# Time-mix recurrence of a two-block token model: the per-head 32x32 operands of two products laid on the diagonal of 128x128 operands by ScalarE

## What is computed

```python
def step(state, inp):
    r_t, d_t, k_t, v_t, kk_t, a_t = inp
    sa = jnp.einsum('bhij,bhj->bhi', state, -kk_t)
    state = (state * d_t[:, :, None, :] + sa[..., None] * (kk_t * a_t)[:, :, None, :]
             + v_t[..., None] * k_t[:, :, None, :])
    return state, jnp.einsum('bhij,bhj->bhi', state, r_t)
```

## Time and profile before

| | us |
|---|---|
| median of three runs (1913.79 to 1920.4) | 1918.26 |
| span of the profiled execution | 1915.1 |
| TensorE matmul busy | 1747.5 (91%) |
| VectorE busy | 1109.7 (58%) |
| ScalarE busy | 656.9 (34%) |
| recurrence stage, from the first L3680 to the end of the last L3694 | 1633.8 to 1670.4 |

### The profile page before, as it was taken

The page is one execution under the profiler, slowest core; times in us unless marked ns, Lnnn a source line. Parts: engine busy times, 40 slices in busy tenths (PEclk is TensorE's granted clock), DMA queues, the critical chain, the costliest instruction groups (busy, mean ns, idle before and its releaser), DMA issues. The chain is left out here.

```text
span 1915.1 us, 30043 instructions
## 1 busy us (share of the span) xinstructions
PE 1747.5 (91%) x12670; PEld 1304.1 (68%) x12670; DVE 1109.7 (58%) x2005; ACT 656.9 (34%) x1042; POOL 0.2 (0%) x4
## 2 busy tenths in 40 slices
PE   6898789988987899999988999999998989799998
PEld 5343256773432588888877788878887877568887
DVE  4342254452332677774478686678667465568765
ACT  3111112331111554452235544464443402145443
POOL 0000000000000000000000000000000000000000
PEclk9799899988997999999988999999999989679999
DMA  9999972289999855524310455545542312035540
GB/s 391 419 420 420 420 308 82 94 329 387 419 421 420 350 177 198 179 97 178 115 67 34 169 191 182 195 158 186 186 174 92 143 43 91 4 154 201 186 163 23
DMA packets 58189, 405.26 MB, mean 212 GB/s; under 512 B 6416, under 2 KB 7824, under 8 KB 10432
## 3 DMA queue, kind: packets, MB, share of 16 engines
q1 hardware_dynamic: 58048, 403.25, 54.4%
HBM read 402.18 MB, written 1.05 MB: 211 GB/s over the span
## 5 line engine op out<-in xcount | busy, mean ns | idle before, releaser
L2110 PE MATMUL ps<-ffn_x,ffn_wh 128*128 128x512 f32 x1408 | 348.3, 400 | 7.8 <-DVE ffn_x L2247 7.4
L2110 PEld LDWEIGHTS ps<-ffn_x,ffn_wh 128*128 128x128 f32 x1408 | 267.3, 193 | 68.3 <-DVE ffn_x L2247 7.7
L2254 DVE TENSOR_TENSOR ffn_wl<-w,ffn_wh 128x2048 fp32r<-128x2048 f32 x132 | 301.5, 2287 | 2.5 <-ACT ffn_wh L2198 1.1
L2198 ACT CAST ffn_wh<-w 128x2048 fp32r<-128x2048 f32 (+1 forms) x140 | 252.9, 1807 | 4.5 <-PEq L726 3.5
L2113 PEld LDWEIGHTS ps<-ffn_x,ffn_wl 128*128 128x128 f32 x1408 | 180.5, 191 | 6.8
L2113 PE MATMUL ps<-ffn_x,ffn_wl 128*128 128x256 f32 x1408 | 183.4, 283 | 0.0
L2213 ACT COPY ffn_part_low<-ps 128x512 f32<-128x512 f32 x88 | 51.5, 586 | 327.7 <-PE ps L2113 327.4
L2258 DVE TENSOR_TENSOR ffn_z<-ps,ffn_part_low 128x512 f32<-128x512 f32 x88 | 60.8, 691 | 149.7 <-ACT ffn_part_low L2213 149.5
L2157 PE MATMUL ps<-ffn_wh,ffn_hidh 128*128 128x512 f32 x352 | 137.7, 391 | 0.6 <-issue 0.6
L2158 PE MATMUL ps<-ffn_wl,ffn_hidh 128*128 128x512 f32 x352 | 137.4, 390 | 0.0
L2159 PE MATMUL ps<-ffn_wh,ffn_hidl 128*128 128x512 f32 x352 | 137.0, 389 | 0.0
(11 more groups left out here) (605 smaller groups left out, 2760.3 us busy)
## 6 DMA issues: line engine op xcount, KB each, us to landing
w<-in_ffn_gu SPq DMA_DIRECT2D x88, 1024.0 KB, 4.8
w<-in_moe_gu SPq DMA_DIRECT2D x60, 1024.0 KB, 22.7
w_extra<-in_moe_gu SPq DMA_DIRECT2D x48, 1024.0 KB, 26.1
w<-in_ffn_dn SPq DMA_DIRECT2D x44, 1024.0 KB, 4.8
w<-in_moe_dn SPq DMA_DIRECT2D x28, 1024.0 KB, 26.3
w_extra<-in_moe_dn SPq DMA_DIRECT2D x21, 1024.0 KB, 27.4
xn<-in_moe_gu SPq DMA_DIRECT2D x10, 1024.0 KB, 26.4
w_extra_late<-in_moe_dn SPq DMA_DIRECT2D x9, 1024.0 KB, 22.8
```

Source lines behind the costliest of these rows:

```text
L2110: return nc.tensor.matmul(pair_of(b)[:, a], high[:, s, tile(a, k)], X[:, k], start=k == 0, stop=False)
L2198: nc.scalar.copy(high[:, n % parts, at], S.buf(units[n])[:, at]).then_inc(*w_high.one())
L2254: nc.vector.tensor_tensor(low[:, s], S.buf(units[n]), high[:, s], ALU.subtract).then_inc(*w_split.one())
```

## The change

ScalarE lays the blocks of four heads on the diagonal of a 128x128 operand: for each quad q it copies all 128 partitions of the block column, scaled by a mask that is 1 on quad q and 0 elsewhere (`K.con(C_QUAD + q, 1)`), to column group q. Off the diagonal stand zeros. For the inverse this goes into a new tile `rw_tm`; for the scores it is done in place in `sc`, over the kinds 0, 2 and 3 that are used up, with kind 1 last after a wait for the other three. There are three calls of `quads_apart`, each of four ScalarE instructions: the inverse of all 32 slots (1024 elements a partition each), the scores of slots 0 to 15 and of slots 16 to 31 (512 elements each). The first two stand in `rwkv_inverse`, the third in the first chunk of `rwkv_chunks`; TensorE waits for the third ahead of chunk 4. L3680 and L3694 become four products each, of a 128x128 stationary operand with 64 columns, in place of sixteen. The last hunk of the diff makes the scratch space for dynamic DMAs smaller, which leaves room for the new tile.

```diff
--- before.py
+++ after.py
@@ -3214,15 +3214,15 @@
             rwkv_factors(K, NormAfterPost(K, post, gain, K.xn[:, :, 1:SEQ + 1]), r, k, sg, a, kk, ar, cl, low, mix_v, by_feat(kp))
             bp = sbi("rw_bp", [P, N_RC, QW])
             sc = sbi("rw_sc", [P, 32, 4, RC])
+            tm_quads = sbi("rw_tm", [P, 32, 4, RC])
             tm = flat(kk)[:, RC * RC:2 * RC * RC]
...
             rows = S.take("ln_rows")
-            rwkv_inverse(K, a, k, r, kk, ar, bp, kp, sc, bon, mix_v, v, g, wv, rows, kv, tm, nv, flat(sg), flat(K.xn))
-            tm = tm.rearrange("p (t u) -> p u t", t=RC)
-            rwkv_chunks(K, ar, cl, bp, kv, sc, tm, nv, y, flat(a), flat(sg))
+            rwkv_inverse(K, a, k, r, kk, ar, bp, kp, sc, tm_quads, bon, mix_v, v, g, wv, rows, kv, tm, nv, flat(sg), flat(K.xn))
+            rwkv_chunks(K, ar, cl, bp, kv, sc, tm_quads, nv, y, flat(a), flat(sg))
             K.retire("rs_made", "sa_ready_a", "kv_made", "kv_taken")
         return rwkv_output(K, y, low, g, rows, flat(K.xn)[:, 0:2 * D], "c_w_o", post_gain)
 
@@ -3458,7 +3458,15 @@
             receptance(7)
 
 
-def rwkv_inverse(K, bt, kt, rk, kend, ar, bp, kp, sc, bon, mix_v, v, g, wv, rows, kv, turned, nv, room, room2):
+def quads_apart(act, K, dst, src, slots):
+
+    for q in (0, 2, 3):
+        last = K.nc.scalar.activation(dst[:, slots, q], src[:, slots], ACT.Copy, scale=K.con(C_QUAD + q, 1))
+    link(act, K.act_step, last)
+    return K.nc.scalar.activation(dst[:, slots, 1], src[:, slots], ACT.Copy, scale=K.con(C_QUAD + 1, 1))
+
+
+def rwkv_inverse(K, bt, kt, rk, kend, ar, bp, kp, sc, tm_quads, bon, mix_v, v, g, wv, rows, kv, turned, nv, room, room2):
 
     nc, S = K.nc, K.stream
     bend = K.sq[:, :, 0:SEQ]
@@ -3597,9 +3605,11 @@
             take_by_values(0)
             take_by_values(1)
             act.wait_ge(*inverted.at(1))
+            quads_apart(act, K, tm_quads, turned.rearrange("p (t u) -> p u t", t=RC), slice(0, 32))
             take_by_values(2)
             take_v(range(4, N_RC))
             take_by_values(3)
+            quads_apart(act, K, sc, sc[:, :, 1], slice(0, 16))
             take_to_state(range(4))
             for n in range(4, 8):
                 take_by_values(n)
@@ -3638,7 +3648,7 @@
             vv.tensor_tensor(g[:], g[:], ln[:, 1:2].to_broadcast([P, N_RC, QW]), ALU.add)
 
 
-def rwkv_chunks(K, ar, cl, bp, kv, sc, tm, nv, y, room, room2):
+def rwkv_chunks(K, ar, cl, bp, kv, sc, tm_quads, nv, y, room, room2):
 
 
     nc = K.nc
@@ -3648,6 +3658,8 @@
         as_made, w_ready, sa_made, sa_ready = K.sig("s_made"), K.sig("s_ready"), K.sig("e_made"), K.sig("p_ready")
         sa_ready_a, rs_made = K.sig("sa_ready_a"), K.sig("rs_made")
         st_made, st_ready, y_made = K.sig("t_made"), K.sig("t_taken"), K.sig("pv_made")
+        y_quads = K.sig("tile_made")
+        whole = lambda of, slot: of[:, slot].rearrange("p q t -> p (q t)")
         quad = lambda q: slice(q * RC, (q + 1) * RC)
         place = [(a, par, q) for a in range(2) for par in range(2) for q in range(4)]
         of_par = K.ps[:, 0:2, :].rearrange("p r (j a i) -> p a r j i", j=4, i=HD)
@@ -3675,9 +3687,8 @@
                 for a in range(2):
                     for par in range(2):
                         g = 2 * a + par
-                        for q in range(4):
-                            w = W[quad(q), g * HD:(g + 1) * HD] if c else nv[0][quad(q), 0, g * HD:(g + 1) * HD]
-                            mm = nc.tensor.matmul(K.ps[quad(q), 2 + a, par * HD:(par + 1) * HD], tm[quad(q), 4 * c + g], w, start=True, stop=True)
+                        w = (W if c else nv[0][:, 0])[:, g * HD:(g + 1) * HD]
+                        mm = nc.tensor.matmul(K.ps[:, 2 + a, par * HD:(par + 1) * HD], whole(tm_quads, 4 * c + g), w, start=True, stop=True)
                     mm.then_inc(*sa_made.one())
                 if c:
                     read_state(c, 1).then_inc(*rs_made.one())
@@ -3689,9 +3700,11 @@
                         mm = nc.tensor.matmul(K.ps[64 * par:64 * par + 64, 4 + q, a * HD:(a + 1) * HD], bp[quad(q), c, g * HD:(g + 1) * HD],
                                               SA[quad(q), g * HD:(g + 1) * HD], start=True, stop=True)
                     mm.then_inc(*st_made.one())
-                for a, par, q in place:
-                    g = 2 * a + par
-                    mm = nc.tensor.matmul(K.ps[quad(q), 2 + a, P + par * HD:P + (par + 1) * HD], sc[quad(q), 4 * c + g, 1], SA[quad(q), g * HD:(g + 1) * HD],
+                if c == 4:
+                    pe.wait_ge(*y_quads.at(1))
+                for g in range(4):
+                    a, par = divmod(g, 2)
+                    mm = nc.tensor.matmul(K.ps[:, 2 + a, P + par * HD:P + (par + 1) * HD], whole(sc, 4 * c + g), SA[:, g * HD:(g + 1) * HD],
                                           start=True, stop=True)
                 mm.then_inc(*y_made.one())
 
@@ -3700,6 +3713,8 @@
             for c in range(N_RC):
                 act.wait_ge(*sa_made.at(2 * c + 2))
                 nc.scalar.copy(SA[:, P:2 * P], K.ps[:, 3, 0:P]).then_inc(*sa_ready_a.one())
+                if c == 0:
+                    quads_apart(act, K, sc, sc[:, :, 1], slice(16, 32)).then_inc(*y_quads.one())
 
         @block.vector
         def _(dve):
@@ -3977,7 +3992,7 @@
     import concourse.bacc as bacc
     from concourse.bass_utils import run_bass_kernel_spmd
 
-    nc = bacc.Bacc("TRN2", target_bir_lowering=False, num_devices=1)
+    nc = bacc.Bacc("TRN2", target_bir_lowering=False, num_devices=1, dynamic_dma_scratch_size=256)
     arrays = {f"in_{n}": a for n, a in layout({n: np.asarray(inputs[n]) for n in INS}).items()}
     ins = {n[3:]: nc.dram_tensor(n, a.shape, F32, kind="ExternalInput").ap() for n, a in arrays.items()}
     out = nc.dram_tensor("out", (P, KT, SEQ), F32, kind="ExternalOutput").ap()
```

## The result

The changed kernel takes 1926.35 us in the median of four runs (1924.18 to 1928.79), the kernel before, measured beside it, 1917.42 (1913.79 to 1920.4): a ratio of 1.0053 (95% interval 1.0040 to 1.0066), slower by 8.9 us. In a later comparison the same kernel took 1927.31 against 1916.7, a ratio of 1.0059 (1.0046 to 1.0072), +10.6. The forecast was +11.1 and 1929.4.

What follows compares the result with a forecast made beforehand. TensorE's path was taken as the bound, with both edited products on the recurrence's serial chain at clock 0.50. Six chunks +7.7, chunks 0 and 7 +1.7 each: 1918.3 + 11.1 = 1929.4 us; 8-in-10 range 1917 to 1934.

Steps and rivals of the forecast that it cites:

- The product: Recurrence, L3680 and L3694: each edited product costs 0.84 us more at clock 0.50, 0.42 more at full clock.
- bounds of 0.79 and 0.92: Extra us per edited product at clock 0.50: 0.79 by L2950's 1.87, 0.92 if the 0.08 overlap is lost too.
- The clock: Recurrence stage: TensorE's clock stays at 0.50, and the 6.9 us at 0.99 of before are lost.
- The sum: Recurrence: chunks go from 4.54 to 6.22 us; six chunks +7.7, chunk 0 +1.7, chunk 7 +1.7, together +11.1 us.
- Both forms of the sum: Recurrence: six chunks at 6.22 us, 37.3, plus chunks 0 and 7; or 16 x 0.84 = 13.4 less 2.4.
- 2.4 of stalls and fast clock: Old recurrence: stalls outweigh the faster middle by 2.38 us over six chunks; the stalls were counted as gone.
- ScalarE's passes: New ScalarE copies in the inverse stage and chunk 0: hidden, at no cost; possible range 0 to +3.7 us, 0 taken.
- upper bound of 1.18 a pass: ScalarE pass over 1024 elements: at most 1.18 us, from a copy of 512 elements taking 0.59; four take 4.7.
- fifth rival: ScalarE's passes show because reading elements 32 apart doubles them: +3.7 us on top, 1933; chance 0.06.
- term of 0: The 0 us entered in the forecast for ScalarE's new passes, out of a range of 0 to +3.7.
- cover of 0.9 us: Inverse stage: `take_v`, which TensorE waits for, is 0.9 us away from the delayed ScalarE queue, so passes stay hidden.
- rival of the clock: Fuller array lifts the clock in nearly all chunks and through the gates: -5.3 and -3.2, -8.5 us, 1909.8; chance 0.07.

Runs made afterwards that it cites:

- columns_16: Changed kernel with both edited products streaming 16 of their 64 moving columns, the rest of the result left out; one run, 1924.74 us.
- the halves: Two variants of the changed kernel, each with only one product 128x128: the one by the inverse 1920.02 us, the scores 1920.21, against 1915.96 before.
- passes_only: Changed kernel with all ScalarE passes, but both products as sixteen 32x32 products on the diagonal blocks; 1915.93 us against 1915.96 before, ratio 0.9999.
- after_filled: Changed kernel plus idle products: six ahead of the recurrence, one in each chunk; 1909.76 us against 1916.7 before (0.9960), repeated 1908.56 against 1917.59 (0.9962).
- filled_and_gates: Changed kernel with idle products ahead of the recurrence, in each chunk, and four of 512 columns behind the gates; 1905.63 us against 1917.59 before, ratio 0.9949.
- before_filled_gates: Kernel before the change with idle products ahead of the recurrence, in each chunk and behind the gates; median 1911.96 us against 1916.21, ratio 0.9995.

## Why the prediction was right, and where it was not

**The product.** +0.84 at clock 0.50 was forecast, from 1.92 - 1.08; measured 1.97 - 1.08 = 0.89, inside the bounds of 0.79 and 0.92. The 1.92 came from L2940, whose loads are these:

```profile
1007.78 1.83 PEld L2940 LDWEIGHTS ps<-cst,dta 128*128 128x128 f32 x8
```

They begin 0.21 ahead of its products (1007.99), under the line before it; the loads of L3691 have nothing to hide under and begin with its products (both at 1645.11). So 1.92 left out most of one load, and had 64 columns more of streaming in its place; 1.97 has all eight. The two nearly cancel, and leave the surplus of 0.05. That the loads pace it is shown by columns_16. That both products stand on the chain is shown by the halves.

**The clock** stayed at 0.50, as forecast, and the 6.9 us at 0.99 were lost. The argument rested on two other stretches with long loads or narrow operands; here the stage itself shows it, at 0.50 with TensorE busy for 42.15 of 46.70 us. The outcome is right and its reason is not shown. The prediction put the 6.9 us at 0.99 down to products that streamed densely ahead of them, but in the timeline of before the chunk ahead of them (from 1643.20) has the same products, the first three as long (0.68, 1.08, 0.68) as in the chunk of the earlier trace rows, which stayed at 0.50. passes_only, with the old products, still has a mean clock of 0.70 in its stage (window below), while the changed kernel and both halves show none above 0.50 behind chunk 0.

```profile
1634.00:1666.00 32.00, 22.32 (x949) 16.65 (x949) 18.44 (x39) 5.73 (x13) 0.00 (x0) 0.70 0.02 4
```

**The sum.** Chunks 6.22 us apart were forecast, 6.33 came; six of them 37.3, measured 38.0 (1637.51 to 1675.51). Both forms of the sum hold: 16 x 0.89 = 14.2, less 2.4 of stalls and fast clock, less some 0.4 in chunk 0 (+1.24 where +1.7 was forecast), whose L3691 was partly at full clock and took 1.33, gives the +11.4 of the stage. No `issue` wait above 0.17 is left in the chunks, as forecast. The spans differ by 11.9; the medians by 8.9 and 10.6.

**ScalarE's passes.** This step failed in its size and held in its outcome. The upper bound of 1.18 a pass came from a copy of neighbouring elements, and the sentence that nothing in the rows made a strided pass slower was no evidence, since none of the rows that it went by was said to be of a strided pass. The passes took 2.0, as the fifth rival had it, and showed as a wait of 1.09, where the prediction expected no wait of TensorE for `take_v` above the old one. Its price of +3.7 was not paid: `take_v` started 2.0 later and not 3.7, the stall behind TensorE's wait of 1.09 was 1.02 smaller, and passes_only puts the total at nothing. That the term of 0 came true is luck, since the cover of 0.9 us that was to bring it about did not hold.

**The base.** Between the forecast of 1929.4 and the median of 1926.35 lie 3.1 us. Of these 0.8 are the base: the forecast added its difference to 1918.26, the median of three runs, and beside the changed kernel the kernel before has 1917.42. The other 2.2 are +11.1 against +8.9, and in the later comparison, with more runs, the difference is +10.6. The 3.2 us between span and median are not all outside the span: the changed kernel's profiled run took 1928.79 with a span of 1927.0, so 1.8 lie outside. The run behind the first profile was therefore one of some 1916.9 and not of 1918.3.

**The rival of the clock** was near in its price for the stage and wrong about what would bring it. It had -5.3 for the chunks, each 4.11; in after_filled the stage is 5.4 shorter, with chunks of 4.07. It had another -3.2 for transposes that start when VectorE is ready and run at full clock; in after_filled they start 2.2 earlier, counted from the end of the stage, and still take 1.97. The sum of -8.5 stands beside -6.9 and -9.0, two comparisons of that kernel. Its full condition, the clock up through the transposes, is met by filled_and_gates alone, which measured -12.0: more than the price. One thing the price left out is the first part of the output product, which takes 3.92 there and 5.97 in after_filled. And it took other work, put into the waits, to lift the clock; the new products alone do not, nor do they keep it.

**Left open.** Why the wait of 1.09 shortened the stalls behind it; why 6.9 us of the old stage were at full clock and none of the new one's; why 32 small loads take less than eight large ones of as many columns; what sets the two groups of before_filled_gates apart; whether less filling in a chunk than 256 columns would do.

## What to carry to other kernels

Sixteen 32x32 products are cheaper than four 128x128 ones while TensorE is at half clock (1.08 against 1.97 us in fp32): the loads of the small ones take 0.84 and those of the big ones 1.78. At full clock the price is 0.68 against 1.10, and here nearly all of the difference lay under VectorE's work (4.02 against 4.07 a chunk); the form with fewer records also had fewer stalls. So read the granted clock of a stage before rewriting its products, and price the rewrite at both levels. A serial stage with short waits of TensorE can be worth filling with idle products. Here filling ahead of the stage alone bought nothing; one idle product in each chunk as well brought the gain, and the wait behind the gates needed a filling of its own.

## What the runs showed that was not expected

- TensorE busy for 90% of a stretch, and at clock 0.50 for all of it, 46.7 us; with one idle product of 256 columns added to each chunk, and some ahead of the stage, it is at 1.00 for all of 31.2 us.
- Eight loads of 128 columns take 0.97 at clock 1.00 and 1.78 at 0.50, and the product with them 1.10 and 1.97. The prediction weighed a rule of the Trainium skill ("TensorE: Matmul & The Clock Gate", section LDWEIGHTS), which has 107 ns for 128 columns. By it eight loads are 0.86, an estimate. The trace is near it at full clock and has twice as much at half clock, so in this kernel the rule holds at full clock only.
- A ScalarE pass over 1024 fp32 elements takes 2.0 us if its elements lie apart on the side it reads or on the side it writes, and 1.06 if neither.
- A new wait of 1.09 us on the engine with the longest busy time cost nothing that could be measured; a stall of its instruction stream behind it was 1.02 shorter.
